# Expert products of 512 columns, a two-expert loop on TensorE and two buffers for gathered rows

## The reference, cut to what matters

```
gate  = sum over the token's two experts of one_hot(expert) * weight        # (tokens, 16)
h     = silu(x @ w_e_gate[e]) * (x @ w_e_up[e])                             # 1024 -> 512, each expert
h     = h * gate[:, e]
moe   = sum over e of h @ w_e_down[e]                                       # 512 -> 1024
x_out = layer_norm(ALPHA * x + moe)
```

## Time and profile before

| what | value |
|---|---|
| median of three runs | 907.18 us (906.63 to 909.52) |
| the profiled execution's own time | 907.86 us |
| its span | 906.5 us |
| TensorE busy (matmul) | 865.3 us, 95% of the span |
| VectorE, ScalarE, GpSimd busy | 427.9, 205.0 and 140.3 us |
| mean granted TensorE clock | 0.991 of full speed |
| expert part (first gathered row block transposed to the end) | 576 to 906 us |

### The profile page before, as it was taken

One profiled execution on the slowest core, in us unless ns is written; L12 is line 12 of the kernel. 1 busy time (PEld: TensorE's weight loads), 2 busy tenths in 40 slices (PEclk: granted clock), 3 DMA queues, 4 the chain that ended last, 5 costly groups with the idle time before them and its releaser, 6 DMA issues.

```text
span 906.5 us, 20900 instructions
## 1 busy us (share of the span) xinstructions
PE 865.3 (95%) x9397; PEld 718.2 (79%) x9397; DVE 427.9 (47%) x863; ACT 205.0 (23%) x310; POOL 140.3 (15%) x131
## 2 busy tenths in 40 slices
PE   7999999999999999999999999999998979999993
PEld 6999888898989999999999988765654655666662
DVE  5653645636575471233232546551312643465556
ACT  4521141311523232322222102120111111121110
POOL 1210000000000001000101011412122333323324
PEclk9999999999999999999999999999999999999997
DMA  9895181461816042321222915699998998999950
GB/s 323 259 287 135 47 279 47 156 217 48 279 47 209 1 155 93 93 94 50 97 87 84 386 72 187 242 353 398 405 376 314 357 328 332 344 365 379 398 202 21
DMA packets 87206, 193.65 MB, mean 214 GB/s; under 512 B 8622, under 2 KB 61590, under 8 KB 78281
## 3 DMA queue, kind: packets, MB, share of 16 engines
q1 hardware_dynamic: 77512, 175.07, 53.7%
q0 software_dynamic: 9600, 17.17, 6.2%
HBM read 171.16 MB, written 36.26 MB: 229 GB/s over the span
## 4 chain that ended last, share of the span: by engine, by line
PE 93%; issue 2%; DVE 2%; DMA 1%; ACT 1%; POOL 1%; SPq 0%; POOLq 0%; DVEq 0%
PE psum L2230 20%; PE psum L466 17%; PE psum L468 16%; PE psum L467 16%; PE psum L2244 9%; PE psum L1934 2%; PE psum L2217 2%; PE psum L1944 2%; PE psum L1973 1%; PE psum L2143 1%; PE psum L2176 1%; PE psum L1959 1%; PE psum L2108 1%; PE psum L2250 1%; DMA xg<-x_rows,idx_i 1%
## 5 line engine op out<-in xcount | busy, mean ns | idle before, releaser
L466 PE MATMUL psum<-x_hi,split_lo 128*128 128x272 f32 x704 | 208.9, 297 | 2.0 <-DVE pbl L1456 1.2
L468 PE MATMUL psum<-x_hi,split_hi 128*128 128x272 f32 x704 | 202.3, 287 | 0.0
L467 PE MATMUL psum<-x_lo,split_hi 128*128 128x272 f32 x704 | 202.2, 287 | 0.0
L2230 PE MATMUL psum<-set,xt 128*32 128x256 f32 x3072 | 185.9, 385 | 14.2 <-issue 12.8
L2230 PEld LDWEIGHTS psum<-set,xt 128*32 128x32 f32 x3072 | 112.1, 111 | 83.1 <-issue 33.5
L466 PEld LDWEIGHTS psum<-x_hi,split_lo 128*128 128x128 f32 x704 | 132.6, 188 | 7.3 <-issue 2.7
L467 PEld LDWEIGHTS psum<-x_lo,split_hi 128*128 128x128 f32 x704 | 132.8, 189 | 1.4 <-issue 1.0
L461 DVE TENSOR_TENSOR split_lo<-raw,split_hi 128x2048 fp32r<-128x2048 f32 x35 | 80.0, 2290 | 113.7 <-ACT split_hi L442 113.2
L468 PEld LDWEIGHTS psum<-x_hi,split_hi 128*128 128x128 f32 x704 | 132.6, 188 | 0.0
L2244 PE MATMUL psum<-set,hT 128*32 128x256 f32 x1536 | 86.6, 380 | 1.5 <-DVE ys L1689 1.5
L2244 PEld LDWEIGHTS psum<-set,hT 128*32 128x32 f32 x1536 | 50.2, 110 | 32.1 <-ACT hT L1089 1.7
(11 more groups left out here) (377 smaller groups left out, 1360.2 us busy)
## 6 DMA issues: line engine op xcount, KB each, us to landing
set<-in_w_e_gate_dram SPq DMA_DIRECT2D x32, 1024.0 KB
set<-in_w_e_up_dram SPq DMA_DIRECT2D x32, 1024.0 KB, 12.5
set<-in_w_e_down_dram SPq DMA_DIRECT2D x32, 1024.0 KB
raw<-in_w_in_dram SPq DMA_DIRECT2D x26, 1024.0 KB, 5.7
cb<-in_state_C_dram SPq DMA_DIRECT2D x8, 1024.0 KB, 7.6
out_dram<-cb SPq DMA_DIRECT2D x8, 1024.0 KB, 5.8
y_group<-x_hi POOLq DMA_DIRECT2D x4, 1152.0 KB, 12.9
kv<-kv_rows SPq DMA_DIRECT2D x4, 1028.0 KB, 7.9
```

Of the source, the lines that this page charges most:

```text
L466: nc.tensor.matmul(out, a_lo, b_hi, start=first, stop=False)
L467: nc.tensor.matmul(out, a_hi, b_lo, start=False, stop=False)
L468: return nc.tensor.matmul(out, a_hi, b_hi, start=False, stop=last)
L2230: last = mm(gate_up()[32 * b:32 * b + 32, j], xt[:, kk, 32 * mine:32 * mine + 32], w, start=kk == 0 and j != 1, stop=kk == KT - 1 and j > 0)
```

## The change

Four edits:

1. In `up` and `down` the blocks b = 0, 1, 2 take 512 of the first 768 columns in one product, then 256; the fourth 32 columns keep products of 256. The columns streamed are the same, the products are 72 and 36 in a turn where they were 96 and 48.
2. TensorE's loop has two turns in its body and runs over t = 2 to 6 (turns 4 to 13), so that it goes back four times: ahead of turns 6, 8, 10 and 12. Turns 1 to 3, 14 and 15 are written out.
3. `xg` has two buffers. POOL issues `gather(n+2)` in its step n, where `gather(n+4)` was issued.
4. ACT scales the rows of expert n+1 in its turn n, one turn ahead, so that `xg` comes free.

```
-            pl.indirect_dma_start(xg[n % 4][0:CAP], None, x1_rows, idx, ...).then_inc(g_in[n % 4], 16)
+            pl.indirect_dma_start(xg[n % 2][0:CAP], None, x1_rows, idx, ...).then_inc(g_in[n % 2], 16)
...
         gather(0)
         pl.wait_ge(idx_ok, 2)
-        for n in range(1, 4):
-            gather(n)
-        pl.wait_ge(idx_ok, 3)
+        gather(1)
         pl.wait_ge(xt_done, 1)
-        gather(4)
+        gather(2)
...
             store_y(n - 1)
-            if n + 4 < NE:
-                if (n + 4) % 4 == 0:
-                    pl.wait_ge(idx_ok, (n + 4) // 4 + 2)
+            if n + 2 < NE:
+                if (n + 2) % 4 == 0:
+                    pl.wait_ge(idx_ok, (n + 2) // 4 + 2)
                 pl.wait_ge(xt_done, n + 1)
                 if n >= FIN0:
                     pl.wait_ge(xs_ok, n - FIN0 + 1)
-                gather(n + 4)
+                gather(n + 2)
...
-            nc.scalar.mul(sums_[n % 4][0:CAP], xg[n % 4][0:CAP], ALPHA).then_inc(xs_ok, 1)
+            nc.scalar.mul(sums_[n % 4][0:CAP], xg[n % 2][0:CAP], ALPHA).then_inc(xs_ok, 1)
...
-            if n >= FIN0:
-                scaled_rows(n)
+            if FIN0 <= n + 1 < NE:
+                scaled_rows(n + 1)
...
         def up(p, loaded, half):
-                for j in range(QB):
-                    for b in range(QB + 1):
-                        mine, at = (b, j) if b < QB else (j, QB)
-                        w = sets[p][:, 2 * half:2 * half + 2, k * DE + at * P:k * DE + at * P + P]
-                        last = mm(gate_up()[32 * b:32 * b + 32, j], xt[:, kk, 32 * mine:32 * mine + 32], w,
-                                  start=kk == 0 and j != 1, stop=kk == KT - 1 and j > 0)
+                w = sets[p][:, 2 * half:2 * half + 2, k * DE:k * DE + DE].rearrange("p q (c n) -> p c q n", c=QB + 1)
+                columns = lambda b: xt[:, kk, 32 * b:32 * b + 32]
+                begin, end_ = kk == 0, kk == KT - 1
+                for b in range(QB):
+                    mm(gate_up()[32 * b:32 * b + 32, 0:2], columns(b), w[:, 0:2], start=begin, stop=end_)
+                for j in range(2):
+                    mm(gate_up()[CAP:P, j], columns(j), w[:, QB], start=begin and j == 0, stop=end_ and j == 1)
+                for b in range(QB):
+                    mm(gate_up()[32 * b:32 * b + 32, 2], columns(b), w[:, 2], start=begin, stop=end_)
+                last = mm(gate_up()[CAP:P, 2], columns(2), w[:, QB], start=begin, stop=end_)
             last.then_inc(gu_done, 1)
...
-        turn(0, 1)
+        turn(0, 1, first=True)
         rows_of(3)
-        turn(0, 2)
+        turn(1, 0)
         rows_of(4)
-        turn(0, 3)
-        with pe.Fori(1, EG - 1) as r:
-            for j in range(4):
-                turn(r, j)
-        for j in range(4):
-            turn(EG - 1, j)
+        turn(1, 1)
+        with pe.Fori(2, NE // 2 - 1) as t:
+            turn(t, 0)
+            turn(t, 1)
+        turn(NE // 2 - 1, 0)
+        turn(NE // 2 - 1, 1, last=True)
```

More of the change, by code:

```diff
@@ L297, in build @@
     cpb = place("cpb", [P, 2, VW], F32, r_xt + NT * DM * 4 + DM * 4)
-    xg, ys, yf, sums_, sets = (xg0, xg1, xg2, xg3), (ys0, ys1), (yf0, yf1), (sum0, sum1, sum2, sum3), (set0, set1)
+    xg, ys, yf, sums_, sets = (xg0, xg1), (ys0, ys1), (yf0, yf1), (sum0, sum1, sum2, sum3), (set0, set1)
     last_hi = place("last_hi", [P, CHUNK], F32R, at_raw)
@@ L369, in build @@
                          "yd_ok", "y_out"))
-    g_in = [sem(f"g_in{i}") for i in range(4)]
+    g_in = [sem("g_in0"), sem("g_in1")]
     ys_out = [sem("ys_out0"), sem("ys_out1")]
@@ L726, in gather @@
             idx = bass.IndirectOffsetOnAxis(ap=idx_i[0:CAP, n:n + 1].bitcast(U32), axis=0)
-            pl.indirect_dma_start(xg[n % 4][0:CAP], None, x1_rows, idx, bounds_check=N - 1, oob_is_err=False
-                                  ).then_inc(g_in[n % 4], 16)
+            pl.indirect_dma_start(xg[n % 2][0:CAP], None, x1_rows, idx, bounds_check=N - 1, oob_is_err=False
+                                  ).then_inc(g_in[n % 2], 16)
         def store_y(n):
@@ L836, in _ @@
                     idx = bass.IndirectOffsetOnAxis(ap=dest_i[0:r, a, i:i + 1].bitcast(U32), axis=0)
-                    pl.indirect_dma_start(xg[2 + a][0:r], None, y_slots, idx).then_inc(ov_in, 16)
+                    pl.indirect_dma_start(yf[a][0:r], None, y_slots, idx).then_inc(ov_in, 16)
                 pl.wait_ge(ov_v, i + 1)
@@ L1797, in _ @@
                 for a in range(2):
-                    step(v.scalar_tensor_tensor(acc, xg[2 + a][0:r], pick[0:r, i, a:a + 1], acc, ALU.mult, ALU.add))
+                    step(v.scalar_tensor_tensor(acc, yf[a][0:r], pick[0:r, i, a:a + 1], acc, ALU.mult, ALU.add))
                 for b in range(2):
@@ L2214, in rows_in @@
             out = wide(0)[:, :, 0:4 * CAP].rearrange("p b (q t) -> p b q t", q=4)
-            cols = xg[e % 4][0:CAP].rearrange("t (p k) -> t k p", k=KT)
+            cols = xg[e % 2][0:CAP].rearrange("t (p k) -> t k p", k=KT)
             for k in range(KT):
@@ L2238, in down @@
                 kk = 2 * half + k
[L2239 to L2245, removed]
+                w = sets[p][:, 4 + half, k * DM:k * DM + DM]
+                columns = lambda b: hT[:, kk, 32 * b:32 * b + 32] if kk < QB else hT[:, b, CAP:P]
+                begin, end_ = kk == 0, kk == QB
+                for b in range(QB):
+                    mm(results()[32 * b:32 * b + 32, 0:512], columns(b), w[:, 0:512], start=begin, stop=end_)
+                for j in range(2):
+                    mm(results()[CAP:P, 256 * j:256 * j + 256], columns(j), w[:, 768:DM], start=begin and j == 0,
+                       stop=end_ and j == 1)
+                for b in range(QB):
+                    mm(results()[32 * b:32 * b + 32, 512:768], columns(b), w[:, 512:768], start=begin, stop=end_)
+                last = mm(results()[CAP:P, 512:768], columns(2), w[:, 768:DM], start=begin, stop=end_)
             last.then_inc(dn_done, 1)
@@ L2271, in _, with turn @@
                             ).then_inc(np_done, 1)
-        def turn(r, j):
-            n, p = 4 * r + j, j % 2
+        def turn(t, odd, last=False, first=False):
+            n = 2 * t + odd
             pe.wait_ge(xt_ok, n + 1)
             for half in range(2):
[L2278 to L2282, removed]
+                up(odd, 16 * t + 16, half)
+            if not last:
+                pe.wait_ge(g_in[1 - odd], 16 * t + 16 + 16 * odd)
+                rows_in(1 - odd)
+            if first:
                 pe.wait_ge(np_ok, 1)
@@ L2288, in turn @@
             for half in range(2):
-                down(1 - p, 32 * r + 16 * ((j - 1) // 2) + 16, half)
+                down(1 - odd, 16 * t + 16 * odd, half)
             pe.wait_ge(hs_ok, n + 1)
             hidden_in()
-        turn(0, 1)
+        turn(0, 1, first=True)
         rows_of(3)
-        turn(0, 2)
+        turn(1, 0)
         rows_of(4)
-        turn(0, 3)
-        with pe.Fori(1, EG - 1) as r:
-            for j in range(4):
-                turn(r, j)
-        for j in range(4):
-            turn(EG - 1, j)
+        turn(1, 1)
[4 more added lines that the diff above has]
+        turn(NE // 2 - 1, 1, last=True)
         pe.wait_ge(ht_ok, NE)
@@ L2316, in _ @@
                 last.then_inc(ix2_done, 1)
-                pe.wait_ge(g_in[0], 16 * j + 16 * (NE // 4 + 1))
+                pe.wait_ge(g_in[0], 16 * j + 16 * (NE // 2 + 1))
                 rows_in(0)
```

## The result

The changed kernel takes 903.06 us (median of 20 runs, 899.81 to 907.75); the kernel before, run beside it, 908.09 (20 runs, 906.54 to 909.91). The ratio is 0.9945 with a 95% interval of 0.9931 to 0.9959: faster by 0.55%. The forecast was 929.5 us, slower; the time lies in its range, near the lower end.

A forecast was written before the change was run, and what follows sets the result against it. It took TensorE's instruction list, at the pace of its columns, as the bound. +20.4 + 1 - 1.8 - 1 + 2.5 + 1.2 = +22.3 on 907.9 us gave 930.2, as a median 929.5; range 900 to 938.

The forecast's parts named there:

- +20.4: TensorE's loop: four jumps back at the old jump's price, 27.2 us, less the old one's 6.8: +20.4 us.
- +1 for bad places: TensorE's loop: unluckily placed jump targets run out before the next block comes, +1 us for all four jumps.
- -1.8 for cover by the gaps: Idle time at the jumps ahead of turns 6, 10 and 12 hides the third indirect DMA's 0.6 us: -1.8 us.
- -6.8: TensorE's loop, a bound: new jumps cost nothing as blocks are held, and the old jump's 6.8 us goes.
- the first two rivals: Instruction blocks stay in: with gathers in time, about 900.5 us, chance 0.21; with gathers late, about 910, chance 0.10.
- The wide products: `up` and `down`: nothing in undisturbed turns, some gain where POOL's DMAs hold records back: -1 us, bounds 0 and -4.4.
- The late gathers: TensorE's `rows_in` waits for gathers, 0.5 us in each of turns 3, 7, 11, 13, 14: +2.5, bounds 0 and 10.
- the second rival: Blocks stay in and gathers are late: nine exposed turns (3, 6, 7, 8, 10 to 14) at 1.05 us, about 910, chance 0.10.
- The third indirect DMA in turns 13 and 14: POOL's step in turns 13 and 14 now has a gather as third indirect DMA: +1.2 us.
- Scaling one turn ahead: ACT's copy stays in the same place of its queue, what follows has slack: 0.
- Unequal widths: Rival for `up` and `down`: the fourth group's narrow products wait for wide ones, 10 us a turn, about 1065, chance 0.03.

The follow-up runs named there:

- e2: The changed kernel with the narrow products of 256 columns, loop of two turns and two buffers kept: 907.81 us, 1.0038 of the kernel before.
- e1: The kernel before with the wide products alone, its loop of four turns and four buffers kept: 894.95 us, 0.9886 of the kernel before.
- e9: The kernel before with the wide products and TensorE's loop written out, four buffers kept: 890.58 us, 0.9798 of the kernel before.
- e5: The kernel before with wide products in `down` alone: 907.48 us, 0.9989 of the kernel before.
- e6: The kernel before with wide products in `up` alone: 897.79 us, 0.9884 of the kernel before.
- e3: The kernel before with two buffers for gathered rows and scaling one turn ahead, old loop and products kept: 918.94 us, 1.0149 of the kernel before.
- e4: The changed kernel with `gather(n+2)` issued ahead of `store_y(n-1)` in POOL's step, not behind it: 890.57 us, 0.9835 of the kernel before.
- e10: e4 with POOL's routing DMAs of `gather_picks` spread over its steps 1 to 9: 889.74 us, 0.9781 of the kernel before.
- e8: e4 with TensorE's loop written out, so that nothing jumps: 892.6 us, 0.9827 of the kernel before.

## Why the prediction was wrong, step by step

**The step that failed** is the one on the loop: "If a jump over 3.8 blocks is served as the one over 9.9 was, four cost 27.2 us", and the reason given for it, "What the rows show is a buffer that has one block in hand after the jump and asks for the next only then. That is how two places would work". The rows showed how a missed jump is served. They didn't show how many old blocks are kept, and a fetch of one block at a time is no evidence on that. Bodies of 3.8 and 5 blocks run with no fetch in 150 us (the changed kernel, e2), bodies of 7.5 and 9.9 with a gap of 4.47 and 4.72 us (e1). So +20.4, +1 for bad places and -1.8 for cover by the gaps fall away, and -6.8 comes in their place (turn 8 loses 7.3 us in the changed kernel, 6.7 from e1 to e9), the bound that the prediction named and gave to the first two rivals. The rule of the Trainium skill in "Runtime: NRT & Kernel Launch", "Instruction fetch mechanics", by which a branch out of the current two blocks waits, is contradicted by these runs. The same section's 2048 instructions for TensorE fit better, but not by themselves: e1's body has 1816 records, weight loads and matmuls together, an estimate of some 1930 instructions at the section's 256 a block and 241 records a block, which is fewer than 2048, and it was fetched anew. A body of 7.5 blocks touches eight or nine of them; whether that is the reason no run shows.

**The wide products** were mis-sized: -1 taken, bounds 0 and -4.4; e1 measures -10.3 (0.0114 x 904.75; 9.8 by the medians) and e2 against the changed kernel -8.4. The first half of the step held: at the pace of the columns there is nothing to gain (e5: -1.0 us with an interval over zero; turns 13 and 14 without their late gathers as long as before), and the gain is where POOL holds the records back (e6). The bound was wrong because the excess of the long turns was counted from 17.9 us, leaving out the 0.6 us of the third DMA in these four turns and in turns 6, 7 and 10 to 12, and because a quarter fewer records were taken to save a quarter of the stretch. With the whole excess, some 17.7 + 0.6 x 9 = 23.1 us, as the base, 9 us are two fifths. The excess of turn 5 also held 1.7 us of half clock (the 0.93 in the earlier trace rows), which the prediction didn't name. And turn 5's 11.5 us of loads, taken as a sign that few records fall into the stretch, tells nothing on what its gaps would be with wider ones.

**The late gathers** were mis-sized: +2.5 taken, bounds 0 and 10; the profiled execution has 9.5. The landing was set between 5.2 and 7.9 us, with 8.9 as the worst; it was 7.1 to 9.2 for the late ones and at most 6.5 in turns 6 and 10. Turns 8 and 12 were exposed with the gaps gone, as the second rival had it, and turns 6 and 10 weren't. The output stores' landings in the same stage were the better row; the first gather's, made nearly alone, said nothing of a gather under the weights' traffic. By the fit of the Trainium skill in "DMA: Bandwidth & Descriptors", "Anatomy of one DMA", it would be an estimate of 2.6 us; every gather that TensorE waited for took 5.2 us or more from issue to use.

**The third indirect DMA in turns 13 and 14**, +1.2 with the old products, is nothing with the wide ones: without their late gathers these turns take 17.4 us. e3, with the old ones, has 17.8 and 18.3, which is +1.4. **Scaling one turn ahead** at 0 left no wait of ACT for a gather or an output store, but it wasn't run by itself. **Unequal widths** run side by side: turn 6 takes 17.35 us with products of 512 and 256 next to each other.

**The rivals.** What came was the second, blocks held and gathers late (0.10, about 910 us), with one term that was too small in all cases: its wide products were 7 to 9 us short, and 910 less 7 to 9 is 901 to 903. That its 9.5 us for late gathers is also the measured 9.5 is luck: it had nine turns at 1.05 each, and it was seven at 0.5 to 2.6. That the time lies in the stated range is owed to the rivals, not to the forecast, whose own range began at 920. By the runs, part by part from the kernel before over e3 and e2 to the changed one, the ratios are +0.0149 for two buffers, -0.0111 for the loop and -0.0093 for the wide products, or +13.5, -10.1 and -8.4 us, which make the measured -5.0; e1 has -10.3 for the wide products on the kernel before. The parts aren't free of each other: a wait ahead of turn 8 can lie in the jump's gap or not, and the longer late gathers (1.7 us and more) took half clock with them in e2 and e3, but not in the changed kernel.

**What stays open.** Why TensorE's instructions come in groups of a few each 0.75 us while POOL issues indirect DMAs: the runs show when, how fast and at what price, not which shared part of the chip does it. The most that is kept of a loop lies between 5 and 7.5 blocks and wasn't narrowed. Why a late gather is followed by half clock in e2 and e3 and not in the changed kernel is open too, and whether the transfers set the pace in e4 and e10.

## What to carry to other kernels

How a missed jump is served doesn't tell how many blocks are held; find the limit by cutting the body in half (one run), and below it take a loop as free (e4 against e8). Where an engine's records thin out with an "issue" ahead of each group while another engine issues indirect DMAs, its list pays by the instruction: put more columns into each there, and expect nothing from it elsewhere. And when buffers are given up, look first at what the transfer now stands behind in its queue: one line moved (e4) was worth twice the whole change. Read the granted clock behind each late transfer as well: in e3's turn 7 it doubled the price of the wait.

## What the runs showed of the hardware that I had not expected

- TensorE holds a loop body of 1196 records (5 blocks) and runs it without a fetch (e2: 57 blocks by q8 where 78 are run); one of 1816 (7.5 blocks) is fetched anew, with 4.5 us of idle time at the jump (e1: 69 blocks by q8, all that are run).
- While POOL issues a run of indirect DMAs, TensorE's weight loads come in groups of one to seven each 0.75 us: 21.2 us of gaps in four turns of the kernel before. It is so at a DMA share of 0.66 (before, 765 to 771) and of 0.98 (changed kernel, 758 to 761).
- A gather of some 68 rows of 4 KB (the mean) that came late took 7.1 to 9.2 us from issue to use beside the weights' transfers in the changed kernel, two others had landed within 6.5, and the first, nearly alone, took 5.2.
- A late gather can cost its wait and half clock on top: 1.71 us of waiting in turn 7 of e3 are followed by some 3.4 us at 0.50, while 2.56 us in turn 7 of the changed kernel leave the clock at 1.00.
